# The recurrence's norm by one matmul of ones, and the value rows' evacuation ahead of a norm's squares

## What is computed

```
o = hgrn2_chunked(...)                                     # (B, S, 8 heads, 128)
o = o * rsqrt(mean(o*o, axis=-1) + 1e-6)
o = o.reshape(B, S, 1024) * hgrn_norm_g * sigmoid(o_gate)
a = o @ w_a
pooled = causal_multiscale_pool(pool_v)                    # 4 groups of 256 channels
b = einsum('bsgc,gcd->bsgd', pooled, w_pool) * pool_scale
merged = sigmoid(gate_a) * a + sigmoid(gate_b) * b
```

## Time and profile before

| what | us |
|---|---|
| median of 3 runs | 1367.7 (1366.07 to 1367.84) |
| the profiled execution, its own time | 1363.8 |
| its span, first to last instruction | 1362.0 |
| TensorE busy | 1211.0 (89% of the span) |
| VectorE busy | 931.7 (68%) |
| ScalarE busy | 521.3 (38%) |
| GpSimd busy | 292.9 (22%) |

### The profile page before, as it was taken

How to read it: one execution, slowest core, us unless ns; L and a number is a source line. 1 busy time by engine, 2 the same in 40 slices (tenths; PEclk the granted TensorE clock), 3 DMA queues, 4 the chain that set the end, 5 groups by cost and what they waited for, 6 DMA issues and landing times.

```text
span 1362.0 us, 17457 instructions
## 1 busy us (share of the span) xinstructions
PE 1211.0 (89%) x6452; PEld 885.4 (65%) x6452; DVE 931.7 (68%) x1815; ACT 521.3 (38%) x959; POOL 292.9 (22%) x261
## 2 busy tenths in 40 slices
PE   6999999999999999999898999898777777878775
PEld 7999998899988899998674555444232222323322
DVE  6765748876664675567687777767777776776655
ACT  4843236545543446645643322323222222222212
POOL 0000000000000000000024445455444444444420
PEclk9999999999999999999999999999999999999999
DMA  7554235544565645348649999999999999999994
GB/s 274 183 172 141 94 110 214 194 152 180 178 228 198 211 165 180 133 179 293 248 192 419 414 420 419 419 420 420 418 421 420 420 419 419 421 420 419 420 421 185
DMA packets 55787, 396.75 MB, mean 291 GB/s; under 512 B 6304, under 2 KB 6304, under 8 KB 8352
## 3 DMA queue, kind: packets, MB, share of 16 engines
q0 software_dynamic: 36864, 268.45, 47.6%
q1 hardware_dynamic: 17136, 119.42, 24.7%
q10 hardware_dynamic: 1712, 7.87, 1.6%
HBM read 394.67 MB, written 1.05 MB: 291 GB/s over the span
## 4 chain that ended last, share of the span: by engine, by line
PE 57%; DMA 28%; DVE 9%; ACT 4%; issue 2%; POOL 0%; DVEq 0%; SPq 0%; POOLq 0%; ACTq 0%
DMA R<-experts,IDX 28%; PE ps L534 25%; PE ps L1063 12%; PE ps L617 10%; PE ps L584 3%; DVE w_lo L1597 2%; PE ps L546 2%; DVE JUNK L2266 1%; PE ps L726 1%; PE ps L714 1%; ACT DIAG L1476 1%; ACT w_hi L1113 1%; PE ps L652 0%; DMA raw<-weights 0%; DVE eq L2243 0%
## 5 line engine op out<-in xcount | busy, mean ns | idle before, releaser
L1063 PE MATMUL ps<-R,DIAG 128*128 128x512 f32 x1020 | 479.4, 616 | 118.6 <-ACT DIAG L1476 118.4
L1063 PEld LDWEIGHTS ps<-R,DIAG 128*128 128x128 f32 x1020 | 189.0, 194 | 387.3 <-issue 195.8
L2420 POOL DMA_INDIRECT R<-experts,IDX x256 | 291.5, 1139 | 548.6 <-PE ps L1063 303.8
L2266 DVE CUSTOM_DVE_ANT_0 JUNK<-R,XN 128x1024 f32<-128x1024 f32 x256 | 313.6, 1225 | 138.7 <-DMA R<-experts,IDX 135.9
L1597 DVE TENSOR_TENSOR w_lo<-raw,w_hi 128x1024 fp32r<-128x1024 f32 x206 | 243.2, 1224 | 98.9 <-ACT w_hi L1113 95.6
L1113 ACT ACTIVATE w_hi<-raw 128x1024 fp32r<-128x1024 f32 x206 | 206.2, 1050 | 89.7 <-DMA raw<-weights 87.2
L534 PE MATMUL ps<-opC_lo,w_hi 128*128 128x256 f32 x544 | 155.3, 286 | 3.7 <-DVE opC_lo L1567 2.4
L534 PE MATMUL ps<-opC_hi,w_hi 128*128 128x256 f32 x544 | 154.7, 284 | 0.0
L534 PE MATMUL ps<-opC_hi,w_lo 128*128 128x256 f32 x544 | 154.6, 284 | 0.0
L1476 ACT ACTIVATE DIAG<-con,coef 128x128 f32<-128x128 f32 x255 | 88.6, 394 | 122.6 <-DVE coef L2276 122.3
L1468 ACT ACTIVATE act_d<-dots 128x2 f32<-128x2 f32 (+1 forms) x130 | 26.3, 203 | 273.6 <-DVE dots L2266 273.5
(11 more groups left out here) (352 smaller groups left out, 1643.4 us busy)
## 6 DMA issues: line engine op xcount, KB each, us to landing
raw<-weights SPq DMA_DIRECT2D x104, 1024.0 KB, 4.8
PQW<-weights SPq DMA_DIRECT2D x6, 1024.0 KB, 8.0
R<-experts,IDX POOLq DMA_INDIRECT x256, 31.4
LNR<-rows ACTq DMA_DIRECT2D x3, 1024.0 KB, 5.1
XF<-xT SPq DMA_DIRECT2D x2, 512.0 KB, 6.2
raw<-weights SPq DMA_DIRECT2D x2, 512.0 KB, 6.9
MEM<-mem ACTq DMA_DIRECT2D x1, 1024.0 KB, 7.7
XR<-x ACTq DMA_DIRECT2D x1, 1024.0 KB, 4.8
```

What stands on the lines that cost most here:

```text
L1063: mm = pe.matmul(psum[:, 4 + 2 * m + n, :], DIAG[:, k, :], rows_[:, D + n * 512:D + (n + 1) * 512], start=(it % 8 == 0 and k == 0), stop=True,
L2266: dve.tensor_tensor_reduce(out=JUNK[:, :], in0=rows_[:, 0:D], in1=XN[:, it // 8, :], scale=1.0, scalar=0.0, op0=ALU.mult, op1=ALU.add, acc ...
L2420: pool.indirect_dma_start(out=R[u][:, :], out_offset=None, in_=experts, in_offset=bass.IndirectOffsetOnAxis(ap=IDX[:, it, k:k + 1], axis=0 ...
```

## The change

The sums of squares are made by four matmuls with ones as the weights and 512 columns of SQ (two heads of 256 tokens), so that they stand on all partitions at once, in banks 4 to 7, from which OG has been taken; all four stand between the halves of gb 3. ScalarE takes the root of each 128x512 (with scale 1/128 and a constant epsilon as bias) into SQ, VectorE the reciprocal of each in place and the product with OG. The head sums, DG, the row broadcasts and their semaphores go. VectorE's list changes: the first two `normed` come right after the pooled low parts, then half of the low part of block 29, then `pool_out` and `o_low` in turn, two more `normed`, the other half of block 29, the last two `pool_out` and `o_low`, and the low part of block 30 after them. On ScalarE the four high parts of o come ahead of the squares of MEM. Later, the evacuation of xv 0 comes ahead of the squares of XR, and the split of q2 0 behind the evacuation of xv 1. One constant (`eps`) is added.

```diff
-            pe.wait_ge(sq_done, 1)
-            dst = free_aux("osum")
-            def head_sums(q):
-                for n in range(8 * q, 8 * q + 8):
-                    mm = pe.matmul(dst[:, n:n + 1], SQ[:, n // MT, n % MT, :], ones[:, 0:1],
-                                   start=True, stop=True)
-                return mm
-            head_sums(0)
-            one("gb", 3, opA, across, mid=lambda: head_sums(1).then_inc(aux_done, 1))
+            def row_sums():
+                pe.wait_ge(sq_done, 1)
+                for j in range(4):
+                    pe.wait_ge(o_taken, 2 * j + 2)
+                    pe.matmul(psum[:, 4 + j, :], ones, SQ[:, 2 * j:2 * j + 2].rearrange("p h m t -> p (h m t)"),
+                              start=True, stop=True).then_inc(o_sums, 1)
+            one("gb", 3, opA, across, mid=row_sums)
...
             pool_groups(0)
-            pe.wait_ge(diag_ready, 1)
-            rms_rows(0)
-            rms_rows(1)
             pool_groups(1)
-            rms_rows(2)
-            rms_rows(3)
...
                     if (st_, j) == ("gb", 2):
-                        act.wait_ge(o_var, 1)
-                        act.activation(st16[:, :], st16[:, :], ACT.Sqrt).then_inc(o_std, 1)
+                        for n in range(4):
+                            act.wait_ge(o_sums, n + 1)
+                            act.activation(SQ[:, 2 * n:2 * n + 2].rearrange("p h m t -> p (h m t)"),
+                                           psum[:, 4 + n, :], ACT.Sqrt, scale=1.0 / P, bias=C("eps")
+                                           ).then_inc(o_std, 1)
                         has_lo(act, "pooled", 3)
                         act.dma_start(XR[:, :, :], x.rearrange("(m p) d -> p m d", p=P)
                                       ).then_inc(xr_in, 16)
...
+            for j in range(4):
+                act.wait_ge(o_ready, j + 1)
+                hi_of(j, OG[:, 2 * j:2 * j + 2, :], opC)
             act.wait_ge(mem_in, 16)
-            act.wait_ge(diag_ready, 1)
             for m in range(MT):
                 st.do(act.activation(SQ[:, 4 * m:4 * m + 4, :, :].rearrange("p a b c -> p (a b c)"),
                                      MEM[:, m, :], ACT.Square, accum_out=msq[:, m:m + 1]))
-            for j in range(4):
-                act.wait_ge(o_ready, j + 1)
-                hi_of(j, OG[:, 2 * j:2 * j + 2, :], opC)
...
-            ahead(BLOCK["q2"])
+            ahead(BLOCK["xkb"])
+            evac("xv", 0, VX[:, :, 0:256], ACT.Copy, further=False)
             for m in range(MT):
...
             scaled(1)
-            for j in range(2):
-                evac("xv", j, VX[:, :, 256 * j:256 * j + 256], ACT.Copy, further=False)
+            evac("xv", 1, VX[:, :, 256:512], ACT.Copy, further=False)
+            ahead(BLOCK["q2"])
...
             ahead_low(28)
             for g in range(4):
                 lo_of(g, PV[:, 2 * g:2 * g + 2, :], opB, "pooled")
-            ahead_low(29)
-            pa = batch(dve, "osum")
-            dve.tensor_scalar(st16[:, :], pa[:, 0:16], 1.0 / P, RMS_EPS, ALU.mult, ALU.add
-                              ).then_inc(o_var, 1)
-            dve.wait_ge(o_std, 1)
-            st.then(dve.reciprocal(st16[:, :], st16[:, :]))
-            drain_aux(dve.tensor_tensor(DG[:, :, :], ident.rearrange("p (a b) -> p a b", a=1)
...
             def normed(j):
-                pa = batch(dve, "obc", j)
-                ins = dve.tensor_tensor(OG[:, 2 * j:2 * j + 2, :], OG[:, 2 * j:2 * j + 2, :],
-                                        v3(pa, 2), ALU.mult)
...
+                dve.wait_ge(o_taken, 2 * j + 2)
+                dve.wait_ge(o_std, j + 1)
+                og, inv = OG[:, 2 * j:2 * j + 2, :], SQ[:, 2 * j:2 * j + 2].rearrange("p h m t -> p h (m t)")
+                st.then(dve.reciprocal(inv, inv))
+                dve.tensor_tensor(og, og, inv, ALU.mult).then_inc(o_ready, 1)
+            def o_low(j):
+                lo_of(j, OG[:, 2 * j:2 * j + 2, :], opC, "o")
+            normed(0)
+            normed(1)
+            low_to[0] = 29
+            low_half(29 % 4, half_end(29, 0), 0)
             wait_stage(dve, "gb", 4)
             pool_out(0)
+            o_low(0)
             pool_out(1)
-            ahead_low(30)
-            normed(0)
-            normed(1)
-            for j in range(2):
-                lo_of(j, OG[:, 2 * j:2 * j + 2, :], opC, "o")
-            pool_out(2)
+            o_low(1)
             normed(2)
             normed(3)
-            for j in range(2, 4):
-                lo_of(j, OG[:, 2 * j:2 * j + 2, :], opC, "o")
+            low_half(29 % 4, half_end(29, 1), 1)
+            pool_out(2)
+            o_low(2)
+            o_low(3)
             pool_out(3)
+            ahead_low(30)
```

More of the change, by code:

```diff
@@ L89 @@
 _a = 0
-for _n, _k in [("kT", 4), ("sc", 4), ("sx", 4), ("U", 2 * NPAIR - 2), ("osum", 1), ("obc", 4), ("memT", 4), ("ln1T", 4),
+for _n, _k in [("kT", 4), ("sc", 4), ("sx", 4), ("U", 2 * NPAIR - 2), ("memT", 4), ("ln1T", 4),
                ("h2T", 4), ("pv0", 1), ("pv1", 1), ("z", 2), ("h3T", 4), ("qTa", 1), ("xpva", 1),
@@ L103 @@
                ("sin", 256), ("invc", 64), ("reset", 256), ("iota", 16),
-               ("zero", 1)]:
+               ("zero", 1), ("eps", 1)]:
     CON[_n] = (_c, _k)
@@ L229, in build @@
         SQ = unit("SQ", 20, [P, HEADS, MT, P])
-        DG = unit("DG", 17, [P, HEADS * MT, P])
         MB = unit("MB", 14, [P, DC, T])
@@ L375, in build @@
         hg_ready, ke2_ready, q2_ready = sem("hg_ready"), sem("ke2_ready"), sem("q2_ready")
[L376 to L379, removed]
+        intra_done, o_done, sq_done, o_taken, o_sums, o_std = (
+            sem("intra_done"), sem("o_done"), sem("sq_done"), sem("o_taken"), sem("o_sums"), sem("o_std"))
+        o_ready, pooled_ready, m_ready = sem("o_ready"), sem("pooled_ready"), sem("m_ready")
         mem_sq, mem_ms, mem_sd, mem_z = sem("mem_sq"), sem("mem_ms"), sem("mem_sd"), sem("mem_z")
@@ L1788, in _ @@
             for h in range(HEADS):
-                st.do(dve.scalar_tensor_tensor(out=OG[:, h, :], in0=psum[:, 4 + h // 2,
-                                               (h % 2) * T:(h % 2 + 1) * T], scalar=V("hg", h),
-                                               in1=OG[:, h, :], op0=ALU.mult, op1=ALU.mult))
+                dve.scalar_tensor_tensor(out=OG[:, h, :], in0=psum[:, 4 + h // 2, (h % 2) * T:(h % 2 + 1) * T],
+                                         scalar=V("hg", h), in1=OG[:, h, :], op0=ALU.mult, op1=ALU.mult
+                                         ).then_inc(o_taken, 1)
             ahead_low(28)
@@ L1816, in normed @@
             def normed(j):
-                pa = batch(dve, "obc", j)
-                ins = dve.tensor_tensor(OG[:, 2 * j:2 * j + 2, :], OG[:, 2 * j:2 * j + 2, :],
-                                        v3(pa, 2), ALU.mult)
-                drain_aux(ins, "obc", j)
-                wait_aux(dve, "obc", j)
-                dve.engine_nop().then_inc(o_ready, 1)
+                dve.wait_ge(o_taken, 2 * j + 2)
[9 more added lines that the diff above has]
+            low_half(29 % 4, half_end(29, 0), 0)
             wait_stage(dve, "gb", 4)
             pool_out(0)
+            o_low(0)
             pool_out(1)
-            ahead_low(30)
-            normed(0)
-            normed(1)
-            for j in range(2):
-                lo_of(j, OG[:, 2 * j:2 * j + 2, :], opC, "o")
-            pool_out(2)
+            o_low(1)
             normed(2)
             normed(3)
-            for j in range(2, 4):
-                lo_of(j, OG[:, 2 * j:2 * j + 2, :], opC, "o")
+            low_half(29 % 4, half_end(29, 1), 1)
+            pool_out(2)
+            o_low(2)
+            o_low(3)
             pool_out(3)
+            ahead_low(30)
             ahead_low(31)
@@ L2489 @@
     put("iota", np.arange(16)[None])
+    put("eps", RMS_EPS)
     pad = np.zeros(512, np.float32)
```

## The result

The changed kernel took 1374.06 us (median of six runs, 1371.94 to 1376.30) against 1366.88 for the kernel before (six runs beside them, 1364.70 to 1369.00): a ratio of 1.0049, interval 1.0032 to 1.0065, so 4 to 9 us slower. The profiled execution took 1372.5 us around a span of 1370.4.

The account below looks back on a forecast made before the run. TensorE was taken to bound the kernel (57% of the chain, gathers' DMA 28%), so delays to it delay the end. Terms 7.6 + 1.5 - 1.4 gave +7.7 us: 1371.5 us profiled, 1375.4 on the median, range 1371 to 1380.

Parts of the forecast that it names:

- The sum: Whole kernel: 7.6 + 1.5 - 1.4 = +7.7 us, giving 1371.5 us profiled and 1375.4 on the median.
- `wa` later by 7.6: Start of `wa`: four VectorE reciprocals of 3.3 us each, all on the path, delay it from 227.42 to 235.05 us.
- The order on VectorE: Two `normed` precede `pool_out(0)`, so TensorE stands inside the pool from 218.8 to 223.1 us.
- The second stop: Ahead of `wa`: TensorE waits from about 226 to 235.05 us for the bank that `pool_out(2)` drains.
- Clock, 1.5: Behind the idle gap ahead of `wa`: a lower granted clock costs 1.5 us, bounded by 0 and twice that.
- Value rows, -1.4: Between xv and xkb: earlier evacuation of xv 0 removes the wait for VX, saving 1.4 us, bounded by 0.
- The cover: Behind xkb's start: q2 0's later split stays hidden, with about 1 us left after h2's first low parts.
- TensorE's part of the norm, 3.4 for 3.4: Between gb 3's halves: four ones matmuls cost 3.4 us, replacing head sums of 3.4, so gain and cost cancel.
- Nothing absorbs the delay: After `wa` 0: VectorE's AM begins 8.5 us later, TensorE is 9.1 late, and no later stage absorbs it.
- The reciprocal is cheap: Rival, VectorE's norm: 0.69 us a reciprocal, `wa` 0.6 us earlier, 1367.2 us or 1365.7 without the clock; chance 0.11.
- A third more an element: Rival, VectorE's reciprocals: long rows cost 8.2 ns an element, 4.3 us each, giving 1379.5 us; chance 0.08.
- The clock stays up: Rival, the gap ahead of `wa`: no clock loss, so +6.2 us, 1373.9 us; chance 0.05.

Follow-up runs that it names:

- E5: Changed kernel plus matmuls whose result nothing reads, filling TensorE's two stops (6 before the pool's third group, 12 before `wa`): 1373.07 us, 1.0044 of before.
- E2: Kernel before with only the value rows' part of the change (xv 0 evacuated earlier, q2 0 split later): 1362.05 us, 0.9992 of before.
- E4: Changed kernel with ScalarE's Abs_reciprocal_sqrt in place of the root, the four VectorE reciprocals removed: 1358.50 us, 0.9971 of before.
- E6: The changed kernel run once more, unaltered: 1376.96 us, 1.0074 of before.
- E7: E4 with VectorE and ScalarE work reordered, all four `normed` ahead of the pool's evacuations, some drains waiting for single pool groups: 1358.53 us, 0.9942 of before.
- E3: Changed kernel with the last two pool evacuations moved ahead of the fourth `normed` on VectorE: 1369.13 us, 1.0049 of before.
- E1: Changed kernel with the value rows as they were before, so the norm's part alone: 1374.10 us, 1.0079 of before.
- E8: The kernel before run once more against itself, unaltered: 1367.40 us, 1.0002.

## Why the prediction was right, step by step

- **The sum.** Forecast +7.7 us in the profiled execution; the stretch that holds the change shows +8.13, the medians +7.2. The stretch is the sum of the terms below, 7.67 + 1.87 - 1.41. The forecast of 1375.4 stands 1.3 above the measured 1374.06; 0.8 of that is the base, 1367.7 in three runs and 1366.88 in six.
- **`wa` later by 7.6.** Counted from the end of the pool's low halves, `wa` starts 14.18 us later before the change and 21.85 after it: **+7.67**. The step that carried it, 3.3 us a reciprocal from three rows of 2, 8 and 16 elements, measured 3.346. From 16 to 512 elements that is (3346 - 253) / 496 = 6.24 ns each: one straight line from 2 to 512. The order on VectorE came as laid out: 4.47 us of TensorE idle inside the pool where 4.3 stood in the text. The second stop was forecast at 9 and is 6.33, with `wa`'s start unmoved: the pool's last two groups ran at the lower clock between the two stops (5.47 us busy where a half takes 2.95; 0.64 over the window with the stop in it), and so took up part of the wait, which the text had said would be hidden.
- **Clock, 1.5.** This is the term that was mis-sized. It measured 24.89 - 23.02 = **1.87**, and E5 took it away whole. The row it was scaled from had a clock of 0.55 for 3.75 us; after 6.33 us of idle it was 0.50 for 4.32. It lies within the bounds of 0 and 3.
- **Value rows, -1.4.** 226.11 instead of 227.52 us from `wa`'s last matmul to xkb: **-1.41**; E2 -1.42. The cover held: VectorE's rows

```profile
487.64 2.36 DVE L1586 TENSOR_TENSOR w_lo<-raw,w_hi 128x1024 fp32r<-128x1024 f32 x2 [1.58 <-ACT w_hi L1099]
489.92 1.86 DVE L1574 SCALAR_TENSOR_TENSOR opC_lo<-ps,vec,opC_hi 128x256 fp32r<-128x256 f32 x4
```

  end 4.7 us (w_lo of q2 0) and 6.5 us (h2's low parts) behind xkb's start, and q2 0 starts 7.5 us behind it: 1.0 us left, where the text had "about 1".
- **TensorE's part of the norm, 3.4 for 3.4.** From the OG product to the pool's first matmul lie 10.58 us before and 10.45 after. The eight records of the ones matmuls stand at 208.68, and gb 3's stop of 0.57 is gone as said.
- **"Nothing absorbs the delay."** Held as far as xkb: VectorE's AM begins 8.4 us later, counted from the OG product (forecast 8.5); from `wa`'s last matmul to the one behind the stop of 2.42 us ahead of `up` lie 33.81 us before and after; and to xkb 226.11 after the change and 226.10 in E2, which has the same value rows and no delay. Behind xkb the traces differ by some us with no change between them (last section), so there only the medians speak: they are 7.2 us apart.

The rivals. *The reciprocal is cheap*: ruled out by 3346 ns; E4 shows what the kernel would do if it were free, and that is faster, as the rival said. *A third more an element*: ruled out by the same row. The Trainium skill's repeat count of 8 ("VectorE: DVE Perf Modes", First the fixed hardware budget), read as eight cycles an element, would be some 4.3 us, an estimate of that page; the trace does not agree with this reading. *The clock stays up*: ruled out by the window of 0.50, and E5, which builds this rival, is 2.0 us shorter in its span than E6. The range of 1371 to 1380 holds the result; its low end is 1.1 us under the terms named for it (1373.9 less 1.8).

What the profile of before could not tell was how near the idea was to a gain. The new norm saves TensorE 3.4 us of broadcasts, and loses because it turns a reciprocal of 16 columns into one of 2048 on the engine that then sets `wa`'s start.

## What to carry to other kernels

Spreading a sum over all partitions with a matmul of ones saves the broadcast, but every later operation then runs at full width: look up the price of each of them per element, and above all the reciprocal's (6.2 ns an element here, against 1.3 for a multiply). Where such an operation sits on the path, take it off that engine first (E4), then lay the order out so that the drains which others wait for stand ahead of it (E7); reordering alone (E3) won only 1.4 us by the end of `wa`, because it moved most of the stop to another place.

## What the runs showed of the hardware that was not expected

**VectorE and GpSimd can hold each other up.** E1's row of 1.09 us instead of 0.17 is not the only one. These are the same GpSimd operation in the kernel before, and VectorE beside it:

```profile
476.75 1.24 POOL L2404 TENSOR_SCALAR_AFFINE_SELECT WS<-WS 128x1024 f32<-128x1024 f32 x1 [476.23 <-DMA BS<-gbs]
...
476.95 3.24 DVE L1597 TENSOR_TENSOR w_lo<-raw,w_hi 128x1024 fp32r<-128x1024 f32 x2
```

The two subtractions took 3.24 us, where the two at 473.37 took 2.36. In E8 they took 3.25 and the GpSimd operation 2.05; in E2 and E4, with VectorE all but idle beside it, it took 1.09. In the changed kernel a VectorE scaling beside it took 1.03 us instead of 0.75. Only in E1 did such a delay reach TensorE.

**The same stop does not always cost the same.** All ten traces have TensorE idle for 2.42 us ahead of `up`. In nine the clock of the 3.75 us behind it was 0.54 to 0.65; in E3 it was 1.00 (window above, 291.74). Stops of 0.97 us and less were followed by no fall in `wa`, nor was the one of 1.26 ahead of xkb in the kernel before. In E4 the clock was still at 1.00 for the 3.11 us between the stops of 1.16 and 1.91, and fell behind the second. It also fell behind 2.12 in E3, 2.19 in E1, and 4.47 and 6.33 after the change.

**A stretch with no change in it can lose 2 us.** From xkb to the first gather lie 219.01 us before, 216.99 after and in E6. The window of the kernel before,

```profile
680.00:685.00 5.00, 4.98 (x30) 5.00 (x31) 3.65 (x9) 3.31 (x10) 0.00 (x0) 0.66 0.01 2
```

and the same window in E8, the same kernel in another execution,

```profile
680.00:685.00 5.00, 4.53 (x40) 4.33 (x40) 3.18 (x9) 3.60 (x13) 0.00 (x0) 1.00 0.00 2
```

show the clock at 0.66 and 1.00 (217.12 us from xkb to the first gather in E8), though the last two stops of TensorE ahead of it, 1.61 and 0.34 us, are the same. E2 (218.55 us) has such a window (0.66 from 656.8 to 661.8), E3 (216.98) none. Why it falls in one execution and not in another is open. Nor do I know whether the OG product's start (204.3 to 205.1 in the six kernels with the new norm in its place, 205.0 to 205.6 in the three with the old one and in E7) is chance: no instruction of the change stands ahead of it. If it isn't, some 0.7 us of the 8.1 come back there.

**The stage of the gathers differs from chip to chip and run to run.** From the first gather to the end: 665.0 us before and 668.1 after in the first two profiles; 664.9 to 665.2 in E1 to E4; 668.3 to 671.9 in E5 to E8, the lowest E7, with the same code. The spans of the 17 runs of the kernel before beside E5 to E8 lie between 1362.7 and 1367.7 us, so two single spans of one kernel can differ by 5 us. And of the 9.3 us that E7's span is below E8's, 2.7 are this stage; its 7.0 in the table, with the interval of the timed runs, is the figure to trust.
